# Three transformer blocks on one core: the last expert unit added by TensorE, the second block's norm scaled after its products, and a shorter gate in the experts

## The reference, cut to what matters

```python
def expert_block(args):                     # block 1: top 4 of 32 experts
    xb, e = args
    u = xb @ w1[e] + b1[e]
    glu = jnp.minimum(u[:, ::2], 7.0)
    lin = jnp.clip(u[:, 1::2], -7.0, 7.0)
    a = glu * jax.nn.sigmoid(1.702 * glu) * (lin + 1.0)
    return a @ w2[e] + b2[e]
y = jnp.zeros((T + 1, D)).at[row_tok].add(yb * row_gate[:, None])

x = x + gt_f * moe(h, ...)                  # end of block 1
x = x * rsqrt(mean(x * x) + EPS) * g_final

hn = x * rsqrt(mean(x * x) + EPS) * attn_norm_g     # start of block 2
proj = hn @ w_in                            # da_q, da_k, da_v, then the rest
```

## Time and profile before

| what | value |
|---|---|
| time, median of 3 runs | 3635.84 us |
| the profiled execution: its time, its span | 3630.8 us, 3629.0 us |
| granted TensorE clock, mean of the span | 0.969 of full speed |
| TensorE matmul, weight load busy | 3391.6 us (93%), 2738.5 us (75%) |
| VectorE, ScalarE, GpSimd busy | 2085.2 (57%), 1764.9 (49%), 1051.8 us (29%) |
| the experts' loop | from about 794 to 2034 us of the span |
| DMA | 696.82 MB, 192 GB/s over the span |

### The profile page before, as it was taken

The page is one execution under the profiler, slowest core; times in us unless marked ns, Lnnn a source line. Parts: engine busy times, 40 slices in busy tenths (PEclk is TensorE's granted clock), DMA queues, the critical chain, the costliest instruction groups (busy, mean ns, idle before and its releaser), DMA issues. The chain is left out here.

```text
span 3629.0 us, 55793 instructions
## 1 busy us (share of the span) xinstructions
PE 3391.6 (93%) x20926; PEld 2738.5 (75%) x20926; DVE 2085.2 (57%) x2480; ACT 1764.9 (49%) x2318; POOL 1051.8 (29%) x435
## 2 busy tenths in 40 slices
PE   7989999989999999999999698899999987789997
PEld 4877777668888888888888584678887856678886
DVE  3320121279999999999999625521153155346665
ACT  3222333257777777777777524432243243133333
POOL 1324222212323232323232240144443300034443
PEclk9999999989999999999999899999999978899999
DMA  8213343359999999999999627123222300013221
GB/s 280 85 59 99 118 137 123 102 192 383 365 382 365 384 362 384 363 383 363 382 363 382 237 77 267 66 90 96 93 93 71 103 32 4 7 59 103 94 93 41
DMA packets 245253, 696.82 MB, mean 192 GB/s; under 512 B 17742, under 2 KB 149570, under 8 KB 186484
## 3 DMA queue, kind: packets, MB, share of 16 engines
q1 hardware_dynamic: 234932, 658.42, 48.9%
q0 software_dynamic: 9936, 36.18, 3.8%
q10 hardware_dynamic: 240, 0.12, 0.0%
HBM read 668.90 MB, written 30.23 MB: 193 GB/s over the span
## 5 line engine op out<-in xcount | busy, mean ns | idle before, releaser
L325 POOL TENSOR_TENSOR split_w<-ring,split_w 128x1024 fp32r<-128x1024 f32 (+1 forms) x294 | 698.2, 2375 | 1618.0 <-ACT split_w L320 1464.8
L2177 DVE TENSOR_TENSOR moe_low<-ring,moe_high 128x2048 fp32r<-128x2048 f32 x408 | 929.4, 2285 | 18.4 <-ACT moe_high L2167 17.4
L2167 ACT ACTIVATE moe_high<-ring 128x1024 fp32r<-128x1024 f32 x810 | 827.6, 1058 | 102.9 <-PE psum L2421 102.8
L320 ACT ACTIVATE split_w<-ring 128x1024 fp32r<-128x1024 f32 (+1 forms) x294 | 304.7, 1037 | 1030.6 <-PE psum L496 600.8
L2417 PE MATMUL psum<-moe_high,moe_xe 128*128 128x512 f32 x2176 | 585.6, 391 | 0.0
L2417 PEld LDWEIGHTS psum<-moe_high,moe_xe 128*128 128x128 f32 x2176 | 410.3, 189 | 83.6
L2328 POOL DMA_INDIRECT moe_y_rows<-moe_ye,moe_target x34 | 197.4, 5807 | 684.3 <-DVE moe_ye L2232 684.3
L496 PE MATMUL psum<-pair,split_w 128*128 128x512 f32 x1488 | 337.9, 389 | 0.0
L2421 PE MATMUL psum<-moe_low,moe_xe 128*128 128x512 f32 x1088 | 336.4, 391 | 0.0
L496 PE MATMUL psum<-b_pair,split_w 128*128 128x512 f32 x1392 | 321.8, 393 | 5.8 <-PEq L1406 2.6
L496 PEld LDWEIGHTS psum<-pair,split_w 128*128 128x128 f32 x1488 | 279.3, 188 | 58.7 <-issue 0.9
(11 more groups left out here) (640 smaller groups left out, 4342.7 us busy)
## 6 DMA issues: line engine op xcount, KB each, us to landing
ring<-in_w_experts SPq DMA_DIRECT2D x408, 1024.0 KB, 7.5
ring<-in_w_mod SPq DMA_DIRECT2D x48, 1024.0 KB, 6.7
ring<-in_w_in SPq DMA_DIRECT2D x39, 1024.0 KB, 5.2
ring<-in_w_up SPq DMA_DIRECT2D x33, 1024.0 KB, 5.1
ring<-in_w_in SPq DMA_DIRECT2D x44, 512.0 KB, 5.2
ring<-in_w_down SPq DMA_DIRECT2D x20, 1024.0 KB, 5.1
ring<-in_w_gate SPq DMA_DIRECT2D x11, 1024.0 KB, 5.3
ring<-in_w_out SPq DMA_DIRECT2D x8, 1024.0 KB, 6.5
```

The costliest lines, as they stand in the source:

```text
L320: self.nc.scalar.activation(high, raw, ACT.Copy).then_inc(self.K.rounded, 1)
L325: self.nc.gpsimd.tensor_tensor(low, raw, high.bitcast(F32), ALU.subtract).then_inc(self.K.split, 1)
L2167: self.nc.scalar.activation(self.B["high"][:, j % HALVES, :], self.raw(j), ACT.Copy).then_inc(self.high, 1)
L2177: self.nc.vector.tensor_tensor(flat(self.low_of(j, 2)), self.K.ring[:, self.ring_slot(j // 2), :], high, ALU.subtract).then_inc(self.low, 2)
```

## The change

In the experts, the gate goes through `Silu` with the scale 1.702, and one product of VectorE takes the place of two: min(silu(1.702 u), limit) times the clamped linear half. The factor 1/1.702 goes on `b_gates`, once, ahead of the experts. The base of the row numbers is subtracted by VectorE (L2211's successor) and the identity matmul L2388 is gone.

Behind the loop, the last unit isn't scattered. SP loads `y_rows` into `x_res` as soon as the scatter before it has landed, ahead of the six chunks of block 2. VectorE makes four one-hot tiles from the last unit's row numbers (`dve_lists`), ScalarE and VectorE split `moe_ye` into high and low, TensorE multiplies them with the one-hot tiles (16 matmuls of 128x512), VectorE adds the result to the 4 tiles of x, and TensorE turns the tiles as they are, without any norm. `enter_turned` evacuates what was turned, scaled by g_final times attn_norm_g per column; these two gains are loaded as columns at the start of the experts, in place of a broadcast of `g_final`.

The factors of both norms, one per token, are computed inside `linear_split` of `b2_qkv` (class `Turnover`), and ScalarE puts the second on the outputs when it evacuates them (4 instructions in place of 1); in `rest_projections` too, where 4 small matmuls bring the factors into a row for `glrT`. The small tables are now loaded and turned as guests of `b2_qkv`, and the bias table is spread by SP at the head of `rest_projections`.

```diff
+    def sp(self, sp):
+        sp.dma_start(self.gain, self.K.A["g_final"].rearrange("(a n) -> a n", a=1).partition_broadcast(P))\
+            .then_inc(self.loaded, 16)
+        self.lam.sp(sp)
+        self.M.sp_bias(sp)
...
+    def act_step(self, sc, j, i):
+        K, nc = self.K, self.nc
+        if (j, i) == (0, 2):
+            K.act_root_table(self.sd[:, 0, :])
+            for n in range(2 * NT):
+                if n >= NT:
+                    sc.wait_ge(self.scaled, n - NT + 1)
+                if n >= 2:
+                    sc.wait_ge(self.squared, n - 1)
+                nc.scalar.activation(self.junk(n), K.x[:, n % NT, :], ACT.Square,
+                                     accum_out=self.sums[:, n // NT, n % NT:n % NT + 1]).then_inc(self.squared, 1)
+            sc.wait_ge(self.summed, 2)
+            nc.scalar.activation(self.sd, self.sums, ACT.Sqrt, scale=1.0 / D).then_inc(self.root, 1)
+        if (j, i) == (0, 3):
+            sc.wait_ge(self.C3.copied, 1)
+            self.M.act_begin(sc)
+            self.lam.act(sc)
+        if (j, i) == (1, 0):
+            sc.wait_ge(self.inverted, 1)
...
+        if (j, i) == (0, 0):
+            self.bias.dve_begin(ve)
+            self.M.dve_constants(ve)
+            ve.wait_ge(self.loaded, 16)
+            for t in range(NT):
+                ve.wait_ge(self.squared, t + 1)
+                nc.vector.tensor_tensor(K.x[:, t, :], K.x[:, t, :], self.gain, ALU.mult).then_inc(self.scaled, 1)
+            self.lam.dve_begin(ve)
+        if (j, i) == (0, 3):
+            ve.wait_ge(self.squared, 2 * NT)
+            nc.vector.tensor_scalar(sums[:, 0, :], sums[:, 0, :], D * EPS, None, ALU.add).then_inc(self.summed, 1)
+            ve.wait_ge(self.summed, 1)
+            nc.vector.scalar_tensor_tensor(sums[:, 1, :], sums[:, 0, :], EPS, sums[:, 1, :], ALU.mult, ALU.add)\
+                .then_inc(self.summed, 1)
+            ve.wait_ge(self.root, 1)
+            nc.vector.reciprocal(self.r[:, 0:2, :], self.sd).then_inc(self.inverted, 1)
+            ve.wait_ge(self.inverted, 1)
+            for t in range(NT):
+                nc.vector.tensor_scalar(K.x[:, t, :], K.x[:, t, :], self.r[:, 0, t:t + 1], None, ALU.mult)\
+                    .then_inc(self.left, 1)
+            self.M.dve_begin(ve)
+            self.lam.dve_end(ve)
...
+def enter_turned(K, dst, pair):
+
+
     with ExitStack() as ctx:
-        N = Norm(K, "b2_norm", ctx, C.cols[:, C.at[key]:C.at[key] + KD], None, dst, pair, xg)
+        N = Norm(K, "b2_norm", ctx, K.mods3[:, 0, :], None, dst, pair, K.x)
         onward = Onward(K, "b2_qkv", "N", pair, N)
-        N.tile = tile
-        sums, sd, r = (K.sb(ctx, f"turnover_{s}", [P, 2, NT]) for s in ("sums", "sd", "r"))
-        junk = lambda t: dst[:, 2 + 2 * (t % 3):4 + 2 * (t % 3), :].rearrange("p a n -> p (a n)")
-        with nc.Block() as block:
-            @block.sync
-            def _(sp):
-                C3.sp(sp)
-                lam.sp(sp)
-                M.sp_bias(sp)
-                bias.sp_spread(sp)
-                bias.sp_end(sp)
-
+        with K.nc.Block() as block:
             @block.gpsimd
             def _(po):
                 onward.low(po, 0)
 
             @block.scalar
             def _(sc):
-                bias.sp_load(sc)
-                C.sp(sc)
+                N.act_evac(sc)
...
                 onward.high(sc)
...
+                pe.nop().then_inc(N.turned, KD)
                 onward.products(pe)
...
-        nc.vector.tensor_scalar(B["source"][:, :], B["ps_place"][:, 0:1], -1.0, None, ALU.mult)
+        nc.vector.scalar_tensor_tensor(B["source"][:, :], B["ps_place"][:, 0:1], -1.0, B["slot_base"], ALU.mult,
+                                       ALU.subtract)
...
         def multiply(c):
-            ve.wait_ge(self.sig, u * 4 + (c + 1))
-            ve.wait_ge(self.clamped, u * 8 + (2 * c + 1))
-            nc.vector.scalar_tensor_tensor(B["glu"][:, c % 2, :], B["sig"][:, c % 2, :], SIG_LIMIT, B["lin"][:, c % 2, :],
-                                           ALU.min, ALU.mult).then_inc(self.clamped, 1)
-            ve.wait_ge(self.clamped, u * 8 + (2 * c + 2))
-            nc.vector.scalar_tensor_tensor(B["a"][:, c % 2, :], self.K.ps[:, c % 2, 0:256], LIMIT, B["glu"][:, c % 2, :],
+            ve.wait_ge(self.glu, u * 4 + (c + 1))
+            ve.wait_ge(self.clamped, u * 4 + (c + 1))
+            nc.vector.scalar_tensor_tensor(B["a"][:, c % 2, :], B["glu"][:, c % 2, :], GLU_LIMIT, B["lin"][:, c % 2, :],
                                            ALU.min, ALU.mult).then_inc(self.act_done, 1)
...
+            nc.scalar.activation(B["glu"][:, c % 2, :], self.K.ps[:, c % 2, 0:256], ACT.Silu, scale=ALPHA)\
+                .then_inc(self.glu, 1)
...
-        nc.tensor.matmul(out, B["eye"][:, :], B["slot_base"][:, :], start=True, stop=False)
         for t in range(NT):
-            ins = nc.tensor.matmul(out, B["pick"][:, t, :], B["gcol"][:, t, :], start=False, stop=(t == NT - 1))
+            ins = nc.tensor.matmul(out, B["pick"][:, t, :], B["gcol"][:, t, :], start=(t == 0), stop=(t == NT - 1))
...
+    def sp_gains(self, sp):
+        K, A = self.K, self.K.A
+        sp.dma_start(K.mods3[:, 0, :], A["g_final"].rearrange("(k p) -> p k", p=P), allow_slow_non_contiguous=True)\
+            .then_inc(self.arrived, 16)
+        sp.dma_start(K.mods3[:, 1, :], A["attn_norm_g_2"][0].rearrange("(k p) -> p k", p=P), allow_slow_non_contiguous=True)\
+            .then_inc(self.arrived, 16)
+
+    def sp_rows(self, sp, n1, y_rows):
+        sp.wait_ge(self.X.scattered, n1 * 16 + 16)
+        sp.sem_inc(self.ready, 1)
+        sp.wait_ge(self.ready, 1)
+        for t in range(NT):
+            sp.dma_start(self.K.x[:, t, :], y_rows[t * P:(t + 1) * P, :]).then_inc(self.arrived, 16)
...
+        for t in range(NT):
+            ins = nc.vector.tensor_scalar(B["pick"][:, t, :], B["iota"], float(t * P), B["place"][:, 0:1], ALU.add, ALU.is_equal)
+        ins.then_inc(self.listed, 1)
...
+    def act_high(self, sc, n1):
+        for m in range(2):
+            sc.wait_ge(self.X.y_ready, n1 * 2 + (m + 3))
+            self.nc.scalar.activation(self.high_of(m), self.y(m), ACT.Copy).then_inc(self.high, 1)
+
+    def dve_rows(self, ve):
+        nc, K = self.nc, self.K
+        for m in range(2):
+            ve.wait_ge(self.high, m + 1)
+            nc.vector.tensor_tensor(self.low_of(m), self.y(m), self.high_of(m).bitcast(F32), ALU.subtract).then_inc(self.low, 1)
+        ve.wait_ge(self.arrived, 32 + 16 * NT)
+        nc.vector.tensor_tensor(K.mods3[:, 0, :], K.mods3[:, 0, :], K.mods3[:, 1, :], ALU.mult)
+        for t in range(NT):
+            ve.wait_ge(self.moved, t + 1)
+            nc.vector.tensor_tensor(K.x[:, t, :], self.out(t).rearrange("p a n -> p (a n)"), K.x[:, t, :], ALU.add)\
+                .then_inc(self.whole, 1)
...
+        def move(t, m, parts):
+            for part in parts:
+                ins = nc.tensor.matmul(self.out(t)[:, m, :], self.B["pick"][:, t, :],
+                                       self.low_of(m) if part else self.high_of(m), start=(part == 0), stop=(part == 1))
+            return ins
+
+        def turn(t, ks):
+            pe.wait_ge(self.whole, t + 1)
+            for k in ks:
+                ins = nc.tensor.transpose(K.ps[:, k, t * P:(t + 1) * P], K.x[:, t, k * P:(k + 1) * P], K.ident[:, :])
+            return ins
+
+        pe.wait_ge(self.listed, 1)
+        pe.wait_ge(self.high, 1)
+        for t in (0, 1):
+            move(t, 0, (0,))
+        pe.wait_ge(self.low, 1)
+        for t in (0, 1):
+            move(t, 0, (1,))
+        pe.wait_ge(self.low, 2)
+        for t in (0, 1):
+            move(t, 1, (0, 1)).then_inc(self.moved, 1)
+        for t in range(NT):
+            turn(t, range(4))
+            if t + 2 < NT:
+                move(t + 2, 0, (0, 1))
+                move(t + 2, 1, (0, 1)).then_inc(self.moved, 1)
+        for t in range(NT):
+            turn(t, range(4, KD))
...
+                L.sp_rows(sp, n1, y_rows)
                 for n in range(last, min(last + RING, len(ring.chunks))):
                     X.wait_low(sp, n1, 2 * (n - last + RING) + 1)
                     K.issue(sp, n)
-                sp.wait_ge(X.scattered, n1 * 16 + 32)
-                sp.sem_inc(y_complete, 1)
-                sp.wait_ge(y_complete, 1)
-                for t in range(NT):
-                    sp.dma_start(K.x[:, t, :], y_rows[t * P:(t + 1) * P, :]).then_inc(K.x_arrived[t], 16)
...
-                X.pool_unit(po, n1, ahead=False)
...
+                bias.sp_spread(sp)
                 K.refill(sp, first, end)
+                bias.sp_end(sp)
...
+                for t in range(NT):
+                    ins = nc.tensor.matmul(ps[0:16, 4, t * P:(t + 1) * P], r[:, 1, t:t + 1].to_broadcast([P, 16]),
+                                           K.ident[:, :], start=True, stop=True)
+                ins.then_inc(row_done, 1)
...
+                    for t in range(NT):
```

(9 more changed lines are left out.)

178 lines of the change are left out of this document (77 added, 101 removed).

## The result

| | before | after | ratio |
|---|---|---|---|
| median of the runs on one chip (6 each) | 3635.8 us (3631.2 to 3637.0) | 3615.6 us (3609.9 to 3620.6) | 0.994, interval 0.9926 to 0.9954 |
| profiled execution: time, span | 3630.8, 3629.0 us | 3614.3, 3612.5 us | |

A forecast was written before the change was run, and what follows sets the result against it. TensorE was taken to set the loop's pace, with VectorE costing it 0.35 us a unit and no DMA waits. 15.2 us (loop) plus 2.4 us (change of blocks) off 3635.8 gave 3618.2 us, range 3611 to 3628 us.

The forecast's parts named there:

- a stall: In the experts' loop, TensorE's turn(3) waits for VectorE behind L2260; the change removes this 0.35 us a unit.
- the next wait: In the experts' loop, without turn(3)'s wait, nothing within the unit is late next; 0.46 us a unit gained in all.
- the end of a block: At the change of blocks, taken as 2.4 us from SP's last issue to the next block's first.
- 18 small loads: At b2_qkv's head TensorE waits for the guests' loads, leaving 3.9 us of the 16.7 gained at the block's start.
- the squares: Rival at the change of blocks: late loads, fourth half chunk waiting behind the squares, 5 us lost, 3626 us; chance 12%.

The follow-up runs named there:

- high_first: The changed kernel with ScalarE's high part of the second half chunk ahead of the evacuation instead of behind it; 3612.8 us (ratio 0.9947).
- all_moves: The changed kernel with the guests' loads early, high part before the evacuation, four small matmuls at b2_qkv's end, one-hot tiles later in the last unit; 3610.6 us.
- after_again: The changed kernel itself run and profiled again, with nothing changed, to see its own scatter; 3610.7 us (ratio 0.9944).
- dma_probe: The changed kernel with the low-weight matmuls of each quarter's first two products covering 128 of 512 columns; 3586.3 us, one run.

## What to carry to other kernels

When a stall is taken out, the next wait can be one that no list of waits showed; look for whatever ends just before an instruction of the bounding engine starts, here 0.3 us. Price the end of a block by the engines that end it and begin the next, not by a queue that waited for something else. A wait that the change creates (TensorE behind 18 small loads) could be moved under work that already ran. Then look at once at what stands next: behind the early loads the squares, harmless until then, took back 3 of 10 us, and the lower clock behind that wait 1.7 more. And one profile doesn't price a stretch behind a gap of TensorE: high_first's theory held only for the first.

## What the runs showed of the hardware

The granted clock behind a short gap is not fixed. The same 24 matmuls of L369, 3.8 us behind the last transposition, took 5.69 us in the first profile of the changed kernel and 7.31 in the second (first lines below). In the five other profiles in which L369 begins at the same T+14.75 they took 7.24 to 8.49, and in high_first and all_moves, which begin it 1.9 us later, 7.18 and 7.78. L677 took 7.0 and 8.5 us, at a clock of 0.81 and 0.65 of the stretch (last line, and the one under after_again):

```profile
2038.80:2044.40 5.60, 5.60 (x24) 4.34 (x24) 5.30 (x9) 4.91 (x9) 0.00 (x0) 1.00 0.00 0
...
2035.40:2042.70 7.30, 7.29 (x24) 5.55 (x24) 5.69 (x9) 5.53 (x9) 1.00 (x1) 0.77 0.00 0
...
2058.15:2065.15 7.00, 7.00 (x26) 5.68 (x26) 6.59 (x14) 4.76 (x9) 0.00 (x0) 0.81 0.47 169
```

The DMA engines of one core moved 386 GB/s for 1100 us (dma_probe), 373 of them loads, and still nobody waited for a landing.
